# Second mixers of a two-block transformer: the inversion of the chunk matrices is interleaved with the last projection tiles, and convolution taps, gating tiles and output rows change places

## What is computed

```python
def hybrid_mix(h, w_in, ...):
    p = h @ w_in
    pa, pb, pc, pd = jnp.split(p, ...)
    y_a = gate_b * causal_depthwise_conv(gate_c * xa, sc_conv_w)      # 3 taps
    y_b = spatial_gating(u, v, sg_w, sg_b, sg_ln_w, sg_ln_b)          # norm of v, 128x128 token mix, times u
    y_c = rwkv7_time_mix(pc, ...)                                     # recurrence over the tokens, 4 heads of 64
    zd = causal_depthwise_conv(z1 * jax.nn.sigmoid(z2), cm_conv_w) + cm_conv_b   # 31 taps
    y_d = jax.nn.silu(layer_norm(zd, cm_ln_w, cm_ln_b))
    return jnp.concatenate([y_a, y_b, y_c, y_d], axis=-1) @ w_out
```

## Time and profile before

| | us |
|---|---|
| median of three runs | 1985.16 |
| the profiled execution, own time | 1986.76 |
| its span in the profile | 1985.0 |
| PE busy | 1951.8 |
| DVE busy | 1188.9 |
| ACT busy | 350.8 |
| POOL busy | 385.8 |

### The profile page before, as it was taken

How to read it: one execution, slowest core, us unless ns; L and a number is a source line. 1 busy time by engine, 2 the same in 40 slices (tenths; PEclk the granted TensorE clock), 3 DMA queues, 4 the chain that set the end, 5 groups by cost and what they waited for, 6 DMA issues and landing times.

```text
span 1985.0 us, 33237 instructions
## 1 busy us (share of the span) xinstructions
PE 1951.8 (98%) x12512; PEld 1496.4 (75%) x12512; DVE 1188.9 (60%) x2291; ACT 350.8 (18%) x836; POOL 385.8 (19%) x485
## 2 busy tenths in 40 slices
PE   8999999999999999999999999999999999999998
PEld 6865994458769944699748859994799568769973
DVE  3453987533639875356754647666776637447674
ACT  1342000011420000300023522000200025421001
POOL 0000205310102063110121810004110404511012
PEclk9999999999999999999999999999999999989999
DMA  8321545534125454354444216444744434125443
GB/s 320 133 86 63 203 170 191 191 106 138 64 106 202 171 191 170 117 204 167 173 157 149 76 40 211 168 168 167 257 167 167 177 142 145 34 96 199 167 173 131
DMA packets 82942, 305.45 MB, mean 154 GB/s; under 512 B 9264, under 2 KB 9392, under 8 KB 82416
## 3 DMA queue, kind: packets, MB, share of 16 engines
q1 hardware_dynamic: 80496, 294.83, 42.1%
q0 software_dynamic: 2304, 8.65, 1.3%
HBM read 302.13 MB, written 1.05 MB: 153 GB/s over the span
## 4 chain that ended last, share of the span: by engine, by line
PE 90%; issue 4%; DVE 3%; ACT 1%; DVEq 1%; ACTq 0%; DMA 0%; POOL 0%; SPq 0%; POOLq 0%
PE psum L451 31%; PE psum L558 22%; PE psum L244 8%; PE psum L1027 7%; PE psum L2590 5%; PE psum L2007 4%; PE psum L463 3%; PE psum L333 3%; PE psum L322 2%; PE psum L1866 1%; PE psum L460 1%; PE psum L288 1%; PE psum L309 1%; PE psum L2976 1%; PE psum L1944 0%
## 5 line engine op out<-in xcount | busy, mean ns | idle before, releaser
L451 PE MATMUL psum<-sq,space 128*128 128x128 f32 x2784 | 345.9, 275 | 1.6 <-DVE sq L655 1.6
L451 PEld LDWEIGHTS psum<-sq,space 128*128 128x128 f32 x2784 | 327.9, 192 | 2.2 <-issue 2.1
L750 POOL TENSOR_TENSOR cat<-space 128x128 f32<-128x128 f32 x76 | 57.8, 761 | 795.9 <-PE psum L558 549.2
L558 PE MATMUL psum<-space,cat 128*128 128x512 f32 x456 | 207.2, 592 | 0.0
L244 PE MATMUL psum<-h,ring 128*128 128x256 f32 x800 | 178.9, 383 | 7.0 <-DMA ring<-in_weights 7.0
L244 PEld LDWEIGHTS psum<-h,ring 128*128 128x128 f32 x800 | 153.1, 193 | 30.3 <-issue 9.7
L558 PEld LDWEIGHTS psum<-space,cat 128*128 128x128 f32 x456 | 86.4, 190 | 109.3 <-issue 109.3
L558 PE MATMUL psum<-ring,space 128*128 128x512 f32 x304 | 141.8, 592 | 0.0
L451 PE MATMUL psum<-h,space 128*128 128x128 f32 x928 | 122.6, 275 | 0.0
L451 PE MATMUL psum<-h,ring 128*128 128x128 f32 x928 | 122.6, 275 | 0.0
L451 PE MATMUL psum<-sq,ring 128*128 128x128 f32 x928 | 120.9, 275 | 0.0
(11 more groups left out here) (440 smaller groups left out, 2930.9 us busy)
## 6 DMA issues: line engine op xcount, KB each, us to landing
ring<-in_weights SPq DMA_DIRECT2D x552, 512.0 KB, 4.1
space<-in_rows POOLq DMA_DIRECT2D x8, 512.0 KB, 4.6
space<-in_gains POOLq DMA_DIRECT2D x6, 512.0 KB, 4.2
const<-in_consts SPq DMA_DIRECT2D x1, 1397.0 KB, 10.7
h<-in_x SPq DMA_DIRECT2D x1, 1024.0 KB, 4.8
x<-in_x_tok SPq DMA_DIRECT2D x1, 1024.0 KB, 15.1
out<-x SPq DMA_DIRECT2D x2, 512.0 KB, 2.6
space<-in_params POOLq DMA_DIRECT2D x2, 509.5 KB, 4.9
```

Of the source, the lines that this page charges most:

```text
L451: last = pe.matmul(out, weights(i), tokens(i), start=(i == 0), stop=(i == 3), skip_group_check=True)
L558: return pe.matmul(k.psum[:, bank, :], lhs, rhs, start=(p == 0), stop=(p == fn.downs - 1), skip_group_check=True)
```

## The change

In `second_tensor` the low-rank step comes after tile 8. Tiles 4 to 13 are computed whole; tiles 14 to 20 in halves of four matmuls (`tile_half`), between which the inversion stands. Tiles 12 to 20 use PSUM banks 6 and 7 alone (`second_bank`), so that each waits for the tile two before it, and banks 0 to 5 are the inversion's. The pair products and the inversion begin right after tile 13. Each product of the inversion is one group of eight matrices in one bank, where it was two groups in two banks. The transposes follow `x1` and `x2`, `spatial` follows tile 18. The output rows come after all tiles, during the chain over the chunks, and three halves each are put between the heads of `out.0` and `out.1`. The tiles of `u`, the factor of `spatial_gating`, are computed last. In `second_vector` the 12 early taps go, and the 16 taps stand in groups of two and three between the masks and sums; in `second_scalar` the sigmoid of tile 10 comes after the decays' exponentials. PE's order behind tile 13 is: pairs `before` and `before_ts`, sum of `vn`, 14a, `p2`, `p2t`, 14b, pair `ak`, `bonus`, `p4`, `p4t`, `n1`, 15a, squares of `vn`, 15b, `p8`, `n2`, 16a, `n3`, 16b, transposes of `vn`, `nd`, 17a, `rb`, `far`, `rk`, 17b, `x1`, 18a, two groups of transposes, `x2`, two more, 18b, `spatial`, `x3`, sum of `zn`, 19a, `na`, `w1`, 19b, `nw`, 20a, squares of `zn`, `s0`, 20b, `u1`, and from there the rows (14a is the first half of tile 14). The number of matmuls, taps, products and additions is the same; a few DVE and ACT instructions are one of 512 elements where they were two of 256.

```diff
+def second_bank(n):
+    return 4 + n % 4 if n < 12 else 6 + n % 2
-PROJ_Z = {7: 1, 9: 0, 11: 10, 12: 11, 13: 12, 14: 13, 15: 4, 16: 5, 17: 6, 18: 7, 19: 8, 20: 9}
+PROJ_Z = {7: 1, 9: 0, 11: 10, 12: 11, 13: 4, 14: 5, 15: 6, 16: 7, 17: 8, 18: 9, 19: 12, 20: 13}
...
+        def tile_half(n, part):
+            if part == 0:
+                free = n - 4 if n < 12 else n - 2
+                pe.wait_ge(k.even_out if n % 2 == 0 else k.odd_out,
+                           w.value("even" if n % 2 == 0 else "odd", free // 2 + 1))
+                opened[n] = pe_take(k, pe, w, P)
+            out = k.bank(second_bank(n))[:, 0, :]
+            for i in range(part * 4, part * 4 + 4):
+                last = mm(out, opened[n][:, i, :], k.h[:, i, :], i == 0, i == KD - 1)
...
+        def prod(label, bank, left, right):
+            for q in range(8):
+                for c in chunks:
+                    last = mm(k.bank(bank, CHUNK)[c, q, :], left[c, q, :], right[c, q, :])
+            last.then_inc(*s.pe.mark(label))
...
+        for n in range(4, 14):
+            tile(n)
+            if n == 8:
+                low_rank()
+        pe.wait_ge(*at(s.dve, "decayed"))
+        chunk_pairs("before", (0, 1), s.bt, s.at)
+        chunk_pairs("before_ts", (2, 3), s.at, s.bt)
...
+        channel_sums("vn", "sum", s.z[:, 10:12, :], 5)
+        tile_half(14, 0)
+        pe.wait_ge(*at(s.dve, "before_ts"))
+        prod("p2", 2, m[1], m[0])
+        prod("p2t", 3, m[0], m[1])
+        tile_half(14, 1)
+        pe.wait_ge(*at(s.dve, "vn.xc"))
+        chunk_pairs("ak", (4, 5), s.kt, s.at)
...
+        prod("p4", 2, m[3], m[2])
+        prod("p4t", 3, m[2], m[3])
+        prod("n1", 0, m[2], s.n[0])
+        tile_half(15, 0)
...
+        channel_sums("vn", "sq", s.vsq, 5)
+        tile_half(15, 1)
...
+        prod("p8", 2, m[1], m[0])
+        pe.wait_ge(*at(s.dve, "n1"))
+        prod("n2", 3, m[0], s.n[1])
+        tile_half(16, 0)
...
+        prod("n3", 0, m[2], s.n[0])
+        tile_half(16, 1)
+        pe.wait_ge(*at(s.dve, "vn"))
...
+        pe.wait_ge(*at(s.dve, "n3"))
...
+        pe.wait_ge(s.product_added, (l + 1) * (ADDED - 1))
+        channel_sums("zn", "sum", s.zd, 0)
...
+        pe.wait_ge(*at(s.act, "zn.std"))
+        pe.wait_ge(*at(s.dve, "yb"))
+        out_part(2, 0, 0)
...
+        token_out(0, 2, (lambda: out_part(0, 0, 1), lambda: out_part(1, 0, 0), lambda: out_part(1, 0, 1)))
...
+        token_out(1, 4, (lambda: out_part(7, 0, 0), lambda: turn_out(0), lambda: out_part(7, 0, 1)))
```

```diff
         tiles_out(9, 11)
-        taps(0, 12)
-        tiles_out(11, 13)
         dve.wait_ge(*at(s.act, "gates"))
...
-        tiles_out(13, 15)
-        centre("vn", s.z[:, 10:12, :], 0)
+        tiles_out(11, 13)
         dve.wait_ge(*at(s.act, "decays"))
...
+        taps(0, 3)
+        masked("before", 0, 1, m[1], "near_st", "before")
+        masked("before_ts", 2, 1, m[0], "near_ts", "before_ts")
...
+        taps(3, 6)
+        masked("ak", 4, 1, m[5], "before_st", "ak")
+        taps(6, 9)
+        add("n1", 0, s.n[0], s.n[1])
...
+        taps(9, 12)
+        tiles_out(15, 17)
+        taps(12, 14)
+        add("n2", 3, s.n[1], s.n[0])
+        taps(14, OWN_TAPS).then_inc(*s.dve.mark("taps"))
+        scaled("vn", "sg_ln_w", "sg_ln_b")
+        add("n3", 0, s.n[0], s.n[1])
```

```diff
         act.activation(s.e_before, s.run_before, ACT.Exp, scale=-DECAY).then_inc(*s.act.mark("decays"))
+        sigmoid_out(10, s.sz[:, 0, :])
+        products(0, 6)
+        tiles_out(12, 14)
+        products(6, 14)
+        copy_bank(2, flat(s.m[2]), "p2")
+        square("vn")
+        tiles_out(14, 16)
+        products(14, 20)
+        copy_bank(2, flat(s.m[0]), "p4")
+        copy_bank(3, flat(s.m[1]), "p4t")
...
```

More of the change, by code:

```diff
@@ L966, in __init__ @@
         self.pe = Steps(sem("mixer_products"), [
[L967 to L971, removed]
+            "lora", "kk_sum", "before", "before_ts", "vn.sum", "p2", "p2t", "ak", "bonus", "p4", "p4t", "n1", "vn.sq",
@@ L975, in __init__ @@
-            "on_std.0", "on_std.1"])
+            "lora", "gates", "kk_std", "decays", "p2", "vn.sq", "p4", "p4t", "vn.std", "p8", "nd", "v_norm_tok", "far",
+            "a_tok", "v_tok", "b_tok", "k_tok", "na", "zn.sq", "gain_g", "zn.std", "yd", "on_std.0", "on_std.1"])
         self.dve = Steps(sem("mixer_elementwise"), [
-            "lora_in", "kk_sq", "zs1", "run", "vn.xc", "decayed", "rkr", "taps", "vn", "bonus", "yb",
-            *tt("before", "far_st"), *tt("before_ts", "ak", "rb"), *tt("rk"), *tt("n0"), *tt("p2t"), *tt("n1"),
@@ L979, in __init__ @@
[L979 to L980 removed]
+            "lora_in", "kk_sq", "zs1", "run", "decayed", "rkr", "before", "before_ts", "n0", "far_st", "vn.xc", "p2t",
+            "ak", "n1", "bonus", "n2", "taps", "vn", "n3", *tt("rb"), *tt("rk"), "x1", "x2", "x3", "zn.xc", "w1", "nw",
+            "s0", "yb", "u1", "s1", "u2", "s2", "zn", "u3", "on_stats.0", "on.0", "yc.0", "on_stats.1", "on.1", "yc.1"])
@@ L1008, in carry @@
     def carry():
-        return mm(k.psum[0:HEAD, 6, 511:512], k.c("ones")[:, 0:HEAD], k.c("ones")[:, 0:1])
+        return mm(k.psum[0:HEAD, 7, 511:512], k.c("ones")[:, 0:HEAD], k.c("ones")[:, 0:1])
     def at(steps, label):
         return steps.at(label, l)
[L1015 to L1024, removed]
     def mm(out, lhsT, rhs, start=True, stop=True):
@@ new lines, in tile, with chunk_pairs @@
+        def tile(n):
+            tile_half(n, 0)
+            tile_half(n, 1)
+        chunks = [slice(CHUNK * c, CHUNK * c + CHUNK) for c in range(2)]
+        m = s.m
+        def chunk_pairs(label, banks, left, right):
+            for q in range(0, 4):
+                for tok_half in range(2):
+                    c = q % 2 * 2 + tok_half
+                    tok = slice(c * CHUNK, c * CHUNK + CHUNK)
+                    for head in range(2):
+                        rows, i = head_rows(q // 2 * 2 + head)
+                        last = mm(k.bank(banks[head], CHUNK)[chunks[tok_half], q, :], left[rows, i, tok],
+                                  right[rows, i, tok])
+            last.then_inc(*s.pe.mark(label))
@@ new lines, in second_tensor @@
+        last.then_inc(*s.pe.mark("v_norm_tok"))
+        pe.wait_ge(*at(s.dve, "n3"))
+        for q in range(8):
+            for c in chunks:
+                last = mm(k.bank(2, CHUNK)[c, q, :], s.n[1][c, q, :], k.c("ident64")[c, :])
+        last.then_inc(*s.pe.mark("nd"))
+        tile_half(17, 0)
+        token_pairs("rb", (0, 1), s.bt, s.rt)
+        pe.wait_ge(*at(s.act, "nd"))
+        prod("far", 3, m[4], m[0])
+        pe.wait_ge(*at(s.act, "v_norm_tok"))
+        token_pairs("rk", (4, 5), s.kt, s.rt)
@@ L1357, in second_scalar @@
         sigmoid_out(8, s.sz[:, 1, :])
-        sigmoid_out(10, s.sz[:, 0, :])
         act.wait_ge(*at(s.pe, "lora"))
```

435 lines of the change are left out of this document (184 added, 251 removed).

## The result

The changed kernel takes 1974.5 us, the median of its runs (1972.3 to 1976.6), against 1985.2 us for the kernel before on the same chip: a ratio of 0.9945, 95% interval 0.9931 to 0.9960. It is 10.7 us faster. The forecast was 1986.7 us, with a range of 1977 to 1994, so both the time and its sign were wrong; rival A's 1973 is the number that came true.

A forecast was written before the change was run, and what follows sets the result against it. The prediction took PE, busy for 98% of the span, to bound the kernel. Waits +11.1, clock -8.6 and filling -1.0 summed to +1.5 us, giving 1986.7 us on the median, with a range of 1977 to 1994.

The forecast's parts named there:

- rival A: Taps run undisturbed or DVE is otherwise some 4 us less late: waits 8.0, clock -12.0, filling -1.0, time 1973; chance 0.22.
- What bounds the kernel: PE, busy 98% of the span; its waits and half clock, 18.9 us, are all to gain unless the array fills better.
- Where DVE starts: First layer: low-rank step one tile earlier, from 1069.4; DVE's scan starts at 1076.8 instead of 1083.8, 7.0 us earlier.
- Wait (1): DVE from the scan to `bt` takes 14.9 us, `decayed` at 1091.7; PE, done with tile 13, waits 0.5 + 1.1 us.
- Wait (2): Behind `decayed`, DVE needs 5.9 us for `rkr`, three taps and two masks, PE has 3.5 of work: wait 2.4 us.
- Wait (3): From the masks to the norm of `vn`, DVE needs 23.6 us, PE has 18.8 to 19: wait taken as 4.3 us.
- Wait (4): `yb` needs tile 20, which leaves PSUM while PE does `u1`: 0.7 us before the first output row.
- ACT and POOL: POOL's additions end at about 1133, PE asks for them near 1141: hidden by 8 us, costing nothing.
- Clock: Half clock in the mixers: 12.0 us lost before, 3.4 after, behind each layer's second inversion wait; token products stay up: -8.6 us.
- Filling: How well PE's array is filled: six row halves now in pairs, fourteen half tiles between small products; -1.0 us, bounds -1.7 and +1.0.
- Sum: Both layers: waits +11.1, clock -8.6, filling -1.0, together +1.5 us; 1986.7 us on the median of the runs.
- under 12 us of waits: Sign that the prediction is wrong: PE's waits summing to under 12 us or over 22; 18.0 was forecast.

## Why the prediction was wrong

- **What bounds the kernel** held. PE stayed busy for 98% of the span, and waits and clock were where the time was. I wrote that waits and clock, 18.9 us, were all there was to gain; 14.1 of them were gained, and 3.9 given back in filling (12.6 and 2.4 with the clock at its estimated price).
- **Where DVE starts** held: the scan comes 7.5 us after the low-rank step's start (1073.3 against 1065.8), forecast 7.4, and the hole of 6.2 us is where the taps had been.
- **Wait (1), the decay chain**: this is the step that failed. I gave the chain its 15.0 us from before, with a few small changes and 0.4 more for an earlier POOL: 14.9. It took 11.5. By my own figures POOL's additions would start 7.2 us after the scan (1084 and 1076.8), where they had started 2.8 us after it before (1086.6 and 1083.8). So less of the chain would run beside them, not more, and the 0.4 had the wrong sign. The length from before held POOL's price: the last two-input operations of the chain took up to 1.2 us in it, and 0.69 each here. The run with the gains' DMA moved had its additions at 7.5 us, about where I put them, and a chain of 13.1. The rest came from something I had misread: in the earlier trace rows I took 4.2 us of idle POOL for a wait for ACT, but it ends 0.2 us behind the landing of the gains' transfer, like the 5.0 us here. That pause put the additions at 12.5 us, after the end of `bt`. The wait forecast here was 1.6, measured none.
- **Wait (2), the masks**: forecast 2.4, measured none. The masks were done at 1089.5 and PE ended its half tile at 1090.5. `decayed` was there 1.8 us before PE asked, and from it to the end of the masks DVE took 4.6 us, not 5.9. With the DMA moved PE waited 1.0 us a layer here.
- **Wait (3), the norm**: forecast 4.3 a layer, measured 1.4 and 2.1, at the place named and for the instruction named. From the masks to the norm's end DVE took 22.5 us, not 23.6: a tap 0.76, not the 0.865 of the earlier trace rows, and the norm 3.6, not 4.2. PE took 20.1 us, not 19, and the masks had left it 1.1 us of room. The price of an operation beside POOL depended on where POOL's operands lie, and the change moved them; with the buffer put back the waits were 6.1 in two places, still below 8.6.
- **Waits (1) to (3) together**, first layer: from the scan to the norm's end I gave DVE 44.4 us and it took 38.7, 5.7 less. The chain is 3.4 of them and the 16 taps, 0.75 us each in the mean, about 1.0. PE took 1.6 us more than I gave it.
- **Wait (4)**: forecast 0.7, measured 0.66. **ACT and POOL** held: POOL's last addition ended at 1123.6, some 6 us earlier than the 1133 I gave it, both counted from the start of the low-rank step.
- **Clock**: -12.0 at its bound (-10.5 by estimate) in place of -8.6. I had a fall behind the norm's wait of 3.2 us in each layer; the waits were 1.4 and 2.1 us and none followed. In the run with the old buffer it came behind 3.3 us, and in one profile of the variants behind 2.0. Falls with no wait ahead, like those at the end of `spatial`, I had not thought of. That the token products stay up with rows between the heads was right, but my reason was half of it: the kernel before with such rows got worse, and the changed kernel with few rows in the chain lost all its gain. It takes rows through the whole chain, and something wide between the inversion's products ahead of it.
- **Filling**: forecast -1.0, by subtraction +3.9 with the clock at its bound and +2.4 at its estimated price: a wrong sign either way. A half tile between small products took 1.8 to 1.9 us from start to start (1088.72 to 1090.54, 1092.56 to 1094.48), where half of 3.45 is 1.73: 28 halves at 0.1 to 0.2 are 2.8 to 5.4 us. The run with three whole tiles a layer didn't confirm that size, so what makes up the rest stays open.
- **Sum**: I had +11.1 - 8.6 - 1.0 = +1.5; it came to -2.1 - 12.0 + 3.9 = -10.2. The term that failed is the waits of PE, 18.0 forecast and 4.8 measured, through a decay chain priced with POOL's additions beside it; the clock's error, the 3.4 for falls behind the norm's waits, hangs on it. The prediction named under 12 us of waits as a sign of being wrong. Rival A had the right time with the right condition, DVE less late by 3 us a layer or more; its reason, undisturbed taps, was not the main one. That its 1973 came so near is in part luck: it had 3.2 us too much of waits, and too little of filling by about as much or more.

## What to carry to other kernels

When small products and wide work are to be distributed, look at every stretch of small ones, and at the waits ahead of it: here the twelve row halves went with 2.4 GHz in one kernel and with 1.2 GHz for 38 us in another, where they came in a slightly different order behind a 3.1 us wait and an uncovered inversion. Wide work moved from one place uncovers it. When an engine's operations are moved beside another's, or away from it, price them by a row with the same neighbour and the same buffers, and look in the diff for buffers that move. Take the work out of a late queue after its last wait for the bottleneck engine, not before it. Where an engine's idle time names "issue", or an engine that was done earlier, look whether a transfer of its own lands at its end.

## What the runs showed of the hardware

- POOL stood still for 5.0 us behind the issue of one DMA of 512 KB (0.59 us), and for 4.9 us in the second layer; with the DMA moved it stood still for 1.2 us and then added. Its next operation, behind a drain, started 0.2 us after the transfer had landed (5.4 us after the issue, and 4.2 to 5.3 in three other places).
- One and the same addition of 128x256 on POOL took 0.73 us with both inputs in one tensor and 0.64 us with one of them in another, and the taps of DVE beside it 0.86 and 0.76 us.
- Around a PE wait of some 2 us in the inversion the clock fell in one profile (2.0 us) and not in another (2.1); it stayed up behind 2.8 and fell at the end of 3.3. At the end of `spatial`, 3.1 us of small products, it fell for 3.4 us in five of the 26 mixers profiled, with no wait ahead. It once stayed down for 38 us, 27 of them with rows and small products much like those through which it stayed up in the changed kernel.
- 32 products of 128x64 took about 1.7 times as long at half clock as at full (5.8 us, and 3.4 by estimate).
